# Hybrid decoder step on one core: steps moved to other places in the engines' hand-written order

## The chip, the cores and the metric

The kernel runs on one core of a Trainium2 chip. The metric is the device time of one launch in microseconds (us), lower is better. Engines as the profile names them: PE (TensorE, with PEld for its weight loads), DVE (VectorE), ACT (ScalarE), POOL (GpSimd) and SP (SyncE). Each runs its own list of instructions in the order in which the program wrote them; they meet only at semaphores. The core has 16 DMA engines.

## The reference, cut to what matters

One decoder layer over 1024 prompt tokens and 8 x 4 sample tokens, all in float32. A mixer (RMSNorm, input projection, a pooling half and a convolution half with 31 taps, LayerNorm, Silu, output projection, residual) comes first; then the expert retrieval, which is most of the time; then a gate with a per-layer embedding, and a last RMSNorm.

```python
def peer block(xk):                                   # 128 tokens
    q = (xk @ w_q).reshape(128, 8 heads, 2, 128)
    s = einsum('thpc,hpkc->thpk', q, sub_keys)
    sv, si = top_k(s, 16)                             # of 128 keys, for both halves
    cand = sv[:, :, 0, :, None] + sv[:, :, 1, None, :]
    top_s, top_j = top_k(cand.reshape(.., 256), 16)
    eidx = take_along_axis(si0 * 128 + si1, top_j)
    gate = softmax(top_s)
    h = gelu(einsum('td,thkd->thk', xk, u_tab[eidx]))  # rows of 1024 floats
    return einsum('thk,thkd->td', gate * h, v_tab[eidx])

h = h + peer(rmsnorm(h, g_ffn))
gate = sigmoid(rmsnorm(h, g_ple) @ w_ple_gate)
h = h + (p @ w_ple_proj) * gate
y = rmsnorm(h, g_final)
```

## The kernel before, in words

A first stage (`front`) runs the mixer for the first 512 prompt tokens and the sample tokens. The second stage (`experts`) does everything else. It walks through 66 blocks, numbered b, of 16 steps each, numbered k. A prompt block is one head of one tile of 128 tokens: block b = 8t + h, so blocks 0 to 63 are the eight prompt tiles, 64 and 65 the sample tokens, packed. A step is one chosen expert of each of the 128 tokens.

For step (b, k) POOL issues an indirect DMA that gathers 128 rows of `u_tab`, 4 KB each, into one of 8 buffers `u_row`, and DVE makes the dot product with the tokens (`dot`, L1772). After the 16 dots ACT makes the gelu of the block (L1277), DVE the coefficients (`coefficients`, L1763, called at k = 2 of the next block), ACT a diagonal matrix for each coefficient (L1188), and PE multiplies that diagonal by the gathered row of `v_tab`, adding in the PSUM bank `acc` (L1671). For a few steps DVE adds the row itself (L1790, `VECTOR_KS`).

POOL's order (L1064 to L1092) is a gather of u for step n, then a gather of v for step n - 20 (`V_BEHIND`). A u gather waits until the dot that used its buffer 8 steps earlier is done. A v gather waits until PE (or DVE) has used its buffer, which held the row 7 steps earlier (`V_RING`). So PE works about 20 steps behind DVE: PE at (b, k) stands level with DVE at (b + 1, k + 4).

When a tile t is complete, PE can't begin the next one in `acc` before `add_sum(t)` on DVE (L1781) has added it to the tokens: L1664 waits for `added`. The first row of tile t on PE is (8t, 0); its last row of the old tile is (8t - 1, 15).

In the gaps of this walk all other work is placed by hand. Tables such as `ADD_AT = {(17, 8): 0, ...}` say at which (b, k) of an engine's loop a step is written:

- The late mixer: the mixer for the other 512 prompt tokens runs within blocks 0 to 20. `LATE_OPEN`, `LATE_GATE`, `LATE_POOL` place steps of the convolution and pooling halves on DVE (`late_open` L1847, `late_gate`, `late_pool` L1873); `PROJECT_AT` the halves of the output projection on PE (L1530); `ADD_AT` the residual additions on DVE (L1926); `SQUARE_AT` their squares on ACT (L1245); four Silu stand at ACT (16, 0).
- Queries for the later tiles: PE multiplies (L1373), ACT copies, DVE picks the best 16 keys (`pick`, L1687 to L1697, called at k = 0 and k = 2).
- DVE ranks the next block's candidates at k = 4 (`rank_tile`, L1703 to L1726).
- The epilogues: `EPILOGUE` lists, for the eight prompt tiles e = 0 to 7, the block in which PE starts the gate of tile e: 40, 42, 44, 48, 50, 52, 59 and 64. PE makes the first half of the gate at k = 8, 11 and 14 of that block (L1429, L1434; for e = 7 at k = 4 and 6) and the second half in the next block. ACT takes the sigmoid of the first half at k = 1 of block + 1 and of the second at k = 8. DVE takes `mix_half` (L1823) of them at k = 7 and 14 of block + 2 and `finish` (L1832) in block + 3.

ACT's loop over b begins with the gelu of block b, which waits for the 16 dots of block b; then it makes the diagonals of block b, while DVE is in block b + 1.

## Time and profile before

| quantity | value |
|---|---|
| median of 3 runs | 3331.15 us (3305.53 to 3348.43) |
| the profiled execution | 3331.15 us |
| its span, first to last instruction | 3329.4 us |
| PE busy | 2669.7 us (80%) |
| DVE busy | 2273.8 us (68%) |
| ACT busy | 806.6 us (24%) |
| POOL busy | 2089.0 us (63%) |
| traffic | 1167.87 MB, of which the gathers 1107.43 MB, mean 351 GB/s |
| mean granted TensorE clock | 0.937 |

How to read it: busy counts the instructions' own time; an engine's idle time matters only where another waits for it. The rows of the timeline give start and duration in us, the engine, the line, the operation, what it writes and reads, the shape and the count of instructions merged; in brackets stands the idle time of the engine before it and what ended it. "remote" is an update that the profile can't assign.

### The profile page before, as it was taken

How to read it: one execution, taken by the hardware profiler on the slowest of the kernel's cores; microseconds unless marked ns; L12 is line 12 of the kernel's file. 1: busy time of each engine (PE TensorE's matmuls, PEld its weight loads, DVE VectorE, ACT ScalarE, POOL GpSimd, SP SyncE). 2: the span in 40 equal slices, each digit the busy share in tenths (PEclk: the TensorE clock that was granted, in tenths of full speed). 3: DMA queues.
4: the chain of work that ended last, by engine and by line, in shares of the span. 5: the costliest groups of instructions: out<-in, count | busy, mean ns of one | idle time of the engine just before them, and what ended most of it. 6: DMA issues, size and time to landing. Idle time of an engine off the chain costs nothing.

```text
span 3329.4 us, 24888 instructions
## 1 busy us (share of the span) xinstructions
PE 2669.7 (80%) x6723; PEld 1218.2 (37%) x6723; DVE 2273.8 (68%) x5244; ACT 806.6 (24%) x1938; POOL 2089.0 (63%) x2169
## 2 busy tenths in 40 slices
PE   8988888788978767677687887699878887778767
PEld 7753434333323323233343442233323333223322
DVE  8867777987875766786765756655566666555545
ACT  2332322223131212111212222222221222212212
POOL 2135666677766767566665666666666666666664
PEclk9998989999999989899898999999999899999899
DMA  5269999999999999899898999999999999999996
GB/s 146 68 223 344 381 369 380 376 392 371 397 367 379 390 372 375 303 379 379 326 383 335 368 366 409 387 373 375 378 372 374 370 371 371 375 373 369 373 367 225
DMA packets 363167, 1167.87 MB, mean 351 GB/s; under 512 B 35401, under 2 KB 88217, under 8 KB 363029
## 3 DMA queue, kind: packets, MB, share of 16 engines
q0 software_dynamic: 304128, 1107.43, 87.2%
q1 hardware_dynamic: 58368, 58.02, 5.3%
q8 instruction: 57, 0.93, 0.1%
q10 hardware_dynamic: 533, 0.83, 0.1%
q14 instruction: 81, 0.66, 0.1%
HBM read 1160.98 MB, written 5.15 MB: 350 GB/s over the span
## 4 chain that ended last, share of the span: by engine, by line
PE 24%; another core or an unknown queue 15%; POOL 14%; DVE 13%; issue 13%; DMA 11%; ACT 4%; POOLq 0%; DVEq 0%; ACTq 0%
PE ex_acc L1671 16%; POOL ex_v_row L1066 8%; POOL ex_u_row L1066 7%; DMA ex_u_row<-in_u_tab_dram,ex_eidx 6%; DMA ex_v_row<-in_v_tab_dram,ex_eidx 5%; DVE ex_u_row L1772 5%; PE ex_q L1373 2%; PE ex_turn L1429 1%; ACT ex_diag L1188 1%; DVE m_mix L1865 1%; PE ex_q L1429 1%; DVE m_hT L1790 1%; PE ex_turn L1510 1%; DVE ex_lists L1690 1%
## 5 line engine op out<-in xcount | busy, mean ns | idle before, releaser
L1671 PE MATMUL ex_acc<-ex_v_row,ex_diag 128*128 128x512 f32 x3840 | 1903.0, 637 | 570.3 <-DMA ex_v_row<-in_v_tab_dram,ex_eidx 252.4
L1772 DVE CUSTOM_DVE_ANT_0 ex_u_row<-ex_u_row,ex_xn 128x1024 f32<-128x1024 f32 x1056 | 1260.5, 1216 | 607.5 <-DMA ex_u_row<-in_u_tab_dram,ex_eidx 459.8
L1066 POOL DMA_INDIRECT ex_v_row<-in_v_tab_dram,ex_eidx x1024 | 996.3, 973 | 638.5 <-issue 260.7
L1671 PEld LDWEIGHTS ex_acc<-ex_v_row,ex_diag 128*128 128x128 f32 x3840 | 729.9, 201 | 1652.0 <-issue 1418.8
L1066 POOL DMA_INDIRECT ex_u_row<-in_u_tab_dram,ex_eidx x1024 | 988.7, 966 | 456.6 <-issue 289.4
L1188 ACT ACTIVATE ex_diag<-m_ident,ex_coef 128x128 f32<-128x128 f32 x948 | 320.2, 393 | 768.9 <-issue 314.3
L1373 PE MATMUL ex_q<-m_mix,m_wq 128*128 128x384 f32 (+3 forms) x832 | 238.5, 441 | 2.3 <-PEq L95 1.9
L1373 PEld LDWEIGHTS ex_q<-m_mix,m_wq 128*128 128x128 f32 x832 | 143.5, 194 | 101.9 <-issue 64.7
L1102 ACT COPY ex_qT<-ex_q 128x384 f32<-128x384 f32 (+3 forms) x50 | 22.0, 440 | 441.9 <-remote 305.2
L1112 ACT ACTIVATE ex_score<-ex_s,ex_rstd 128x128 f32<-128x128 f32 (+1 forms) x144 | 42.3, 364 | 237.6 <-remote 130.6
L1790 DVE SCALAR_TENSOR_TENSOR m_hT<-ex_v_row,ex_coef,m_hT 128x1024 f32<-128x1024 f32 x76 | 97.4, 1281 | 0.0
L1384 PE MATMUL ex_s<-m_keysT,ex_qT 128*128 128x128 f32 x288 | 49.8, 309 | 56.3 <-ACT ex_qT L1102 46.6
L1510 PE MATMUL ex_turn<-m_hT,m_wq 128*128 128x512 f32 x192 | 86.3, 592 | 0.0
L1772 DVE DVE_READ_ACCUMULATOR2_ANT ex_hdot<- 128x1 f32 x1056 | 85.6, 81 | 0.4 <-issue 0.4
L1277 ACT ACT_TABLE_LOAD x65 | 83.4, 1283 | 1.2
L1865 DVE SCALAR_TENSOR_TENSOR m_mix<-m_mix,m_taps 128x512 f32<-128x512 f32 x109 | 82.1, 753 | 0.0
L1118 ACT ACT_TABLE_LOAD x63 | 80.8, 1283 | 1.1
L1384 PEld LDWEIGHTS ex_s<-m_keysT,ex_qT 128*128 128x128 f32 x288 | 41.3, 202 | 88.6 <-ACT ex_qT L1102 59.2
L1277 ACT ACTIVATE ex_hact<-ex_hdot 128x16 f32<-128x16 f32 x66 | 14.2, 216 | 239.8 <-issue 122.8
L1429 PE MATMUL ex_turn<-m_mix,m_wq 128*128 128x512 f32 x128 | 60.3, 615 | 6.2 <-ACT m_wq L1142 6.2
L1694 DVE MAX8 ex_lists<-ex_same 128x8 f32<-128x128 f32 (+1 forms) x144 | 32.7, 281 | 41.0 <-remote 28.0
L1429 PE MATMUL ex_q<-m_mix,m_wq 128*128 128x512 f32 x128 | 57.7, 594 | 0.0
(371 smaller groups left out, 1968.0 us busy)
## 6 DMA issues: line engine op xcount, KB each, us to landing
m_wq<-in_w_q_dram SPq DMA_DIRECT2D x18, 1024.0 KB
ex_u_row<-in_u_tab_dram,ex_eidx POOLq DMA_INDIRECT x1024
ex_v_row<-in_v_tab_dram,ex_eidx POOLq DMA_INDIRECT x1024
fr_w<-in_w_in_dram SPq DMA_DIRECT2D x12, 512.0 KB, 4.4
m_wq<-in_w_in_dram SPq DMA_DIRECT2D x6, 1024.0 KB
m_wq<-in_w_out_dram SPq DMA_DIRECT2D x4, 1024.0 KB
m_mix<-in_w_ple_gate_dram SPq DMA_DIRECT2D x8, 512.0 KB
out_y_prompt_dram<-m_wq SPq DMA_DIRECT2D x7, 512.0 KB
```

The source lines that it names most:

```text
L1066: pool.indirect_dma_start(out=row[:, :], out_offset=None, in_=table, in_offset=bass.IndirectOffsetOnAxis(ap=picks(b)[:, k:k + 1], axis=0)) ...
L1118: nc.scalar.activation(expo[r % KEPT][:, :], shift[r % 2][:, :], ACT.Exp, accum_out=norm[r % KEPT][:, :]).then_inc(exped, 1)
L1188: nc.scalar.activation(diag[:, n % DIAGS, 0:rows(t)], pattern[:, :], ACT.Copy, scale=coef[b % 2][:, k:k + 1]).then_inc(diaged, 1)
L1277: nc.scalar.activation(hact[b % 2][:, :], hdot[b % 2][:, :], ACT.Gelu_apprx_tanh).then_inc(gelued, 1)
L1373: last = nc.tensor.matmul(q_ps[:, out:out + cols], weights(load, c), xg[:, c, at:at + cols], start=(c == 0), stop=(c == DC - 1))
L1384: last = nc.tensor.matmul(s_ps[0:rows(t), j * P:(j + 1) * P], qT[:, s % 2, j * P:j * P + rows(t)], keysT[:, half, :], start=True, stop=True)
L1429: last = nc.tensor.matmul(gate_out[:, :], x2T[:, c, :], w_gate[:, c, cols], start=(c == 0), stop=(c == DC - 1))
L1510: last = nc.tensor.matmul(late_bank[n % 2], weights(late_load(n), c), late_h[:, c, :], start=(c == 0), stop=(c == DC - 1))
L1671: last = nc.tensor.matmul(acc[0:rows(t), half, :], diag[:, tensor_sums(n) % DIAGS, 0:rows(t)], row[:, half * HALF_D:(half + 1) * HALF_D], ...
L1772: nc.vector.tensor_tensor_reduce(out=u_row[n % U_RING][:, :], in0=u_row[n % U_RING][:, :], in1=xn[:, :], scale=1.0, scalar=0.0, op0=ALU.mu ...
L1790: ins = nc.vector.scalar_tensor_tensor(out=tokens, in0=row[:, :].rearrange("p (c e) -> p c e", c=DC), scalar=coef[b % 2][:, k:k + 1], in1= ...
L1865: nc.vector.scalar_tensor_tensor(out=u, in0=src, scalar=tap[:, j:j + 1], in1=u, op0=ALU.mult, op1=ALU.add).then_inc(late_tapped, 1)
```

## The change

All edits move steps to other (b, k) places; what a step computes stays. `add_sum(t - 1)` goes from k = 5 to k = 2 of the second block of a tile, behind the coefficients and ahead of the second pick. The sigmoid of the first gate half goes from k = 1 of block + 1 to k = 15 of the epilogue's own block, on ACT, behind the block's last diagonal and ahead of the next block's gelu. `mix_half` goes from k = 7 and 14 to 3 and 12, `take_spread` from 14 to 11. In the late mixer `LATE_OPEN`, `LATE_GATE` and `LATE_POOL` move up by one or two steps in the entries shown, the additions by 3 to 5 steps, the squares by 2 to 6, the four Silu from ACT (16, 0) to (15, 15), three halves of the projection by 1 or 2 steps.

```diff
-LATE_OPEN = ((8, 0), (9, 10), (11, 14), (13, 4))
-LATE_GATE = ((8, 5), (9, 15), (12, 3), (13, 9))
-LATE_POOL = ((10, 6), (10, 14), (13, 14), (14, 8))
+LATE_OPEN = ((8, 0), (9, 10), (11, 13), (13, 2))
+LATE_GATE = ((8, 5), (9, 15), (12, 2), (13, 7))
+LATE_POOL = ((10, 6), (10, 14), (13, 12), (14, 6))
-PROJECT_AT = {(15, 5): (0, 0), (15, 9): (1, 0), (16, 3): (0, 1), (16, 6): (1, 1), (16, 8): (2, 0), ...
+PROJECT_AT = {(15, 5): (0, 0), (15, 9): (1, 0), (16, 1): (0, 1), (16, 4): (1, 1), (16, 7): (2, 0), ...
-ADD_AT = {(17, 8): 0, (17, 11): 1, (17, 15): 2, (18, 6): 3, (18, 12): 4, (19, 2): 5, (19, 9): 6, (19, 15): 7}
-SQUARE_AT = {(16, 11): 0, (16, 14): 1, (17, 2): 2, (17, 9): 3, (17, 15): 4, (18, 5): 5, (18, 12): 6, (19, 1): 7}
+ADD_AT = {(17, 3): 0, (17, 6): 1, (17, 12): 2, (18, 3): 3, (18, 9): 4, (18, 15): 5, (19, 6): 6, (19, 12): 7}
+SQUARE_AT = {(16, 6): 0, (16, 9): 1, (16, 14): 2, (17, 6): 3, (17, 12): 4, (18, 2): 5, (18, 9): 6, (18, 14): 7}
@@ ACT, late_step
-                if (b, k) == (16, 0):
+                if (b, k) == (15, 15):
                     for c in range(MC):
@@ ACT, the loop over blocks
                         if k == TURN_AT[e][1] + 1 and e < N_TILES - 1:
                             embedding_out(e)
-                    if rest_e is not None and k == 1:
-                        sigmoid_half(rest_e, 0)
+                        if k == TOPK - 1:
+                            sigmoid_half(e, 0)
@@ DVE, late_step
-                if (b, k) == (20, 6):
+                if (b, k) == (20, 2):
                     late_sum_squares(DC - 1)
@@ DVE, the loop over blocks
                         if b - 1 in VECTOR_KS:
                             dve.wait_ge(coefed, b)
-                    if k == 5 and t > 0 and h == 1:
-                        add_sum(t - 1)
+                        if t > 0 and h == 1:
+                            add_sum(t - 1)
                     if k == 0 and s is not None:
                         pick(s)
...
-                    if k == 14 and t == N_TILES - 1 and h == 2:
+                    if k == 11 and t == N_TILES - 1 and h == 2:
                         take_spread()
                     dot(b, k)
...
-                    if mix_e is not None and k == 7:
+                    if mix_e is not None and k == 3:
                         mix_half(mix_e, 0)
-                    if mix_e is not None and k == 14:
+                    if mix_e is not None and k == 12:
                         mix_half(mix_e, 1)
                         add_mixed(mix_e)
```

## Rows read from the trace of the kernel before

**Rows 1.** Busy time by windows: us; PE, PEld, DVE, ACT, POOL; PEclk; DMA share, GB/s.
```profile
217.00:3266.00 3049.00, 2424.79 (x5700) 1045.69 (x5699) 2069.81 (x4833) 720.27 (x1743) 2020.01 (x2087) 0.93 0.97 371
627.00:1178.00 551.00, 461.83 (x1005) 189.97 (x1004) 426.34 (x801) 143.00 (x344) 385.67 (x383) 0.95 1.00 384
1005.00:1035.00 30.00, 24.43 (x53) 10.82 (x54) 17.42 (x28) 4.51 (x9) 17.55 (x19) 0.84 0.90 334
1382.00:1412.00 30.00, 15.90 (x50) 8.55 (x50) 23.83 (x44) 2.83 (x9) 12.84 (x14) 0.77 0.68 244
1770.00:1800.00 30.00, 16.02 (x47) 8.62 (x48) 20.24 (x41) 3.38 (x11) 12.29 (x14) 0.72 0.66 233
...
3240.00:3305.00 65.00, 46.00 (x92) 13.35 (x92) 37.42 (x45) 10.45 (x21) 39.01 (x36) 0.84 0.86 307
```

**Rows 2.** Waits of the whole program: who waited for whom, us, times, longest.
```profile
POOL ex_v_row L1066 <- PE ex_acc L1671: 232.4, 129, 9.3
...
POOL ex_u_row L1066 <- DVE ex_hdot L1772: 78.9, 79, 5.7
```

**Rows 3.** Timeline where tile 2 begins (block 17).
```profile
999.62 2.50 PE L1671 MATMUL ex_acc<-ex_v_row,ex_diag 128*128 128x512 f32 x4 [1.96 <-issue]
1010.57 6.95 PE L1671 MATMUL ex_acc<-ex_v_row,ex_diag 128*128 128x512 f32 x11 [8.45 <-remote]
...
993.63 0.23 DVE L1763 SCALAR_TENSOR_TENSOR ex_coef<-ex_expo,ex_norm,ex_hact 128x16 f32<-128x16 f32 x1
...
1005.60 1.21 DVE L1781 TENSOR_TENSOR m_hT<-m_hT,ex_acc 128x1024 f32<-128x1024 f32 x1
```

**Rows 4.** Timeline where tile 3 begins (block 25).
```profile
1369.93 0.23 DVE L1763 SCALAR_TENSOR_TENSOR ex_coef<-ex_expo,ex_norm,ex_hact 128x16 f32<-128x16 f32 x1
...
1374.16 1.96 PE L1671 MATMUL ex_acc<-ex_v_row,ex_diag 128*128 128x512 f32 x4 [0.60 <-DMA ex_v_row<-in_v_tab_dram,ex_eidx]
...
1375.95 5.32 PE L1373 MATMUL ex_q<-m_mix,m_wq 128*128 128x384 f32 x16
...
1378.95 0.48 DVE L1694 MAX8 ex_lists<-ex_same 128x8 f32<-128x128 f32 x2 [6.09 <-remote]
...
1385.94 1.22 DVE L1772 CUSTOM_DVE_ANT_0 ex_u_row<-ex_u_row,ex_xn 128x1024 f32<-128x1024 f32 x1 [4.29 <-remote]
...
1388.83 0.93 POOL L1066 DMA_INDIRECT ex_u_row<-in_u_tab_dram,ex_eidx  x1 [5.66 <-DVE ex_hdot L1772]
...
1396.10 5.75 PE L1671 MATMUL ex_acc<-ex_v_row,ex_diag 128*128 128x512 f32 x8 [14.83 <-DVE m_hT L1781]
...
1400.15 0.94 POOL L1066 DMA_INDIRECT ex_v_row<-in_v_tab_dram,ex_eidx  x1 [7.91 <-PE ex_acc L1671]
```

**Rows 5.** Timelines of two epilogues: block 44 (the first two rows), block 52.
```profile
2269.81 0.23 DVE L1763 SCALAR_TENSOR_TENSOR ex_coef<-ex_expo,ex_norm,ex_hact 128x16 f32<-128x16 f32 x1
...
2273.30 1.88 PE L1434 MATMUL ex_turn<-m_keysT,ex_qT 128*128 128x512 f32 x4
...
2637.09 0.23 DVE L1763 SCALAR_TENSOR_TENSOR ex_coef<-ex_expo,ex_norm,ex_hact 128x16 f32<-128x16 f32 x1
...
2645.75 1.88 PE L1434 MATMUL ex_turn<-m_keysT,ex_qT 128*128 128x512 f32 x4
...
2647.53 1.21 DVE L1772 CUSTOM_DVE_ANT_0 ex_u_row<-ex_u_row,ex_xn 128x1024 f32<-128x1024 f32 x1
...
2658.15 0.94 POOL L1066 DMA_INDIRECT ex_u_row<-in_u_tab_dram,ex_eidx  x1 [0.30 <-issue]
```

**Rows 6.** Timeline where the sample tokens begin (block 65).
```profile
3232.41 1.95 PE L1671 MATMUL ex_acc<-ex_v_row,ex_diag 128*128 128x512 f32 x4 [1.36 <-issue]
...
3240.97 1.22 DVE L1781 TENSOR_TENSOR m_hT<-m_hT,ex_acc 128x1024 f32<-128x1024 f32 x1 [6.16 <-remote]
```

**Rows 7.** The page's groups: the table load ahead of the gelu; busy, mean ns, idle.
```profile
L1277 ACT ACT_TABLE_LOAD x65 | 83.4, 1283 | 1.2
```

**Rows 8.** One line's account: what DVE waited for ahead of L1926, us, times.
```profile
  remote: 30.4, 3
```

More of the change, by code:

```diff
@@ L790 @@
 TAP_ADD_AT = (15, 7)
-PROJECT_AT = {(15, 5): (0, 0), (15, 9): (1, 0), (16, 3): (0, 1), (16, 6): (1, 1), (16, 8): (2, 0), (16, 10): (2, 1), (16, 13): (3, 0),
+PROJECT_AT = {(15, 5): (0, 0), (15, 9): (1, 0), (16, 1): (0, 1), (16, 4): (1, 1), (16, 7): (2, 0), (16, 10): (2, 1), (16, 13): (3, 0),
               (17, 1): (3, 1), (17, 4): (4, 0), (17, 7): (4, 1), (17, 10): (5, 0), (17, 13): (5, 1), (18, 1): (6, 0), (18, 4): (6, 1),
               (18, 7): (7, 0), (18, 10): (7, 1)}
-ADD_AT = {(17, 8): 0, (17, 11): 1, (17, 15): 2, (18, 6): 3, (18, 12): 4, (19, 2): 5, (19, 9): 6, (19, 15): 7}
-SQUARE_AT = {(16, 11): 0, (16, 14): 1, (17, 2): 2, (17, 9): 3, (17, 15): 4, (18, 5): 5, (18, 12): 6, (19, 1): 7}
+ADD_AT = {(17, 3): 0, (17, 6): 1, (17, 12): 2, (18, 3): 3, (18, 9): 4, (18, 15): 5, (19, 6): 6, (19, 12): 7}
+SQUARE_AT = {(16, 6): 0, (16, 9): 1, (16, 14): 2, (17, 6): 3, (17, 12): 4, (18, 2): 5, (18, 9): 6, (18, 14): 7}
 def col(t):
```

## The prediction

> **What bounds the kernel now.** Read the table by windows first. From the first dot of the expert stage at 217 us to the last at 3266 us, 1056 rows of u and nearly as many of v are gathered, and the DMA engines are busy 0.97 of the time at 371 GB/s; PE is busy 2425 and VectorE 2070 of those 3049 us [rows 1]. So the gathers set the pace, 3049/1056 = 2.9 us for a pair of rows, and a change of schedule can give back only time in which they were not fed: at most 0.03 of 3049, about 91 us, and part of that is how a saturated stretch reads. See there too how uneven the idle time is: 1.00 over the whole late mixer stage, 0.68 and 0.66 in two stretches of 30 us.
>
> Then the waits: who stops feeding the DMAs? POOL issues every gather. It waited 232 us for PE to free a v buffer and 79 us for a dot to free a u buffer [rows 2]. So the buffers are the clock, and PE's progress counts for more than VectorE's.
>
> Then the timelines at the low stretches. At each new tile of tokens PE must not start its sum before VectorE has taken the old sum out of acc (L1781). In a common case PE ends its last row at 1002.1, VectorE adds at 1005.6, PE resumes at 1010.6 after 8.45 us of idleness [rows 3]. At tile 3 it is worse: PE ends its row at 1376.1 and runs a query; VectorE is held in its second pick (waits of 6.09 and 4.29 us), makes two dots and a ranking and then adds, 1.2 us before PE resumes at 1396.1 after 14.83 us idle. POOL pauses 5.66 us for the dot and 7.91 us for PE [rows 4]. The stretch 1382:1412 loses (0.97 - 0.68) x 30 = 8.7 us against the mean, 1770:1800 (tile 4) 9.3 and 1005:1035 (tile 2) 2.1 [rows 1]. The 13.6 us of POOL pauses thus cost 0.64 us of DMA time each.
>
> The releases of some waits come microseconds after the record of the releasing instruction ended (VectorE's 6.09 us wait in a chain of its own instructions [rows 4]). I can't name the cause; it goes into the range.
>
> **The change, part by part.** No instruction is added or removed; every edit moves a step, with its waits, to another place in its engine's order. No DMA is issued from a moved step, and POOL's and SP's orders stay.
>
> *add_sum from k = 5 to k = 2.* v row (8t-1, 15), the last of the old tile, is issued behind u row (8t+1, 3), since v lags by 20 rows. VectorE at k = 2 is therefore early and waits for PE: in [rows 3] from 993.9, the end of the coefficients, to 1002.1, so 8.2 us, then adds 1.2. Its dots 2 and 3 and the ranking come later, and the dots have room: POOL issues the gather that reuses a buffer several us after its dot, 9.4 us in the row pair of [rows 5] (dot (52,4) ends 2648.7, the gather into its buffer starts 2658.15). An 8.2 us delay just fits, so a common seam costs nothing in dots and frees PE 3 to 7 us sooner. What it can win is only what the stretch lost, 2.1 us at tile 2, and no other of tiles 1, 5, 6 and 7 has a low stretch of this kind; together I take 2 us of gain (0 to 4).
> At tile 3, and tile 4 alike, the add would start at 1376.1 instead of 1394.9; PE's query (to 1381.3) hides it, PE resumes 14.8 us sooner and the 7.91 us pause goes. What is late next is dot 2, now behind the add: the pick began right behind the coefficients, at 1370.2, and would begin behind the add, at 1377.3, 7.1 us later. Without its two long waits (10.4 us) the dot comes at 1382.6, before POOL stopped (1383.2), and the 5.66 us pause goes too (all 8.7 us back); stretched as before, it comes at 1393.0, the pauses sum to 12.8 instead of 13.6 and 0.5 us comes back. Nothing before shows this order, so I take the middle, 5 us, twice: 10 us (1 to 18).
> At tile 8 PE ends its last row at 3234.4 and the add is at 3241.0, 6.6 us later [rows 6]. Behind it hang the last epilogue and the last sums, and 3240:3305 loses (0.97 - 0.86) x 65 = 7.2 us [rows 1]. I take 4 us (0 to 7.2).
>
> *The first sigmoid half from (block+1, k = 1) to (block, k = 15).* This speaks against the change. It now stands ahead of the next block's gelu on ScalarE, and it waits for PE's gate product. Behind the gelu wait the coefficients on VectorE at k = 2, and behind those its dots. In epilogue 4 the coefficients were made at 2637.1 and the gate product ended at 2647.6; with a gelu table load of 1.28 [rows 7] and 1.2 for the sigmoid, the gelu and the hand-overs (each a short activation, my estimate from the 0.7 us of a 128x512 step) they can't come before 2650.1, 13.0 us later. Room at dot 4 was 9.4, and mix_half at k = 3 takes 0.7 of it: POOL pauses 4.3 us more. In epilogue 1 the gate ends at 2275.2, the coefficients were at 2269.8, and the shift is 7.9 us: inside the room [rows 5]. Three of the seven are of the long kind, the rest near the short one. PE meets the next block's first diagonal two rows behind the gate, some 3 us, so it is hardly late itself. Cost: 0 if the pauses fall where POOL waits for PE anyway, 3 x 4.3 x 0.64 = 8 us if none does; I take 3. In the last epilogue the sigmoid ahead of the last gelu is harmless only if the tile-8 add is early.
> At this point the Trainium skill (ScalarE: Activation LUTs, What ACT_TABLE_LOAD costs) says that a switch of tables takes a 1.28 us load and a 1.38 us drain. The trace agrees on the load (1283 ns [rows 7]); no row here shows the drain. By the page each shift would be an estimated 1.4 us longer, and the sum 3 x 1.4 x 0.64 = 3 us higher.
>
> *mix halves to k = 3 and k = 12, take_spread to k = 11.* The first can't wait, since its sigmoid precedes the coefficients. The others come two or three rows before PE has worked them off, up to 8 us of VectorE waiting inside the same room: 0.
>
> *The late mixer's places.* Adds, squares, openings and pools come one to five rows earlier; PE's products hardly move. PE at row (b, k) is level with VectorE at (b+1, k+4). An add for the product at PE (16, 1) is thus due at (17, 5); it stood at (17, 8) and now stands at (17, 3), so VectorE waits two pairs more, 5.8 us, eight times over. The three longest such waits before summed to 30.4 us [rows 8], and the DMAs still ran at 1.00 of 627:1178 [rows 1]. Nothing can be gained at 1.00. Cost 0 to 6 us (one pair at two of its places); I take 2. If that cover is gone each add costs its wait.
>
> Sum: -(2 + 10 + 4) + 3 + 2 = -11. The profiled execution took 3331.15 us, its span 3329.4, and it is the median of the runs shown. Forecast 3320.
>
> **The rivals.**
> *No gain.* The pick is as stretched as before, so dot 2 takes the place of PE as POOL's wait at tiles 3 and 4 (2 us gained), the other terms give 3, the costs of 5 stand: 3331. For it: the two waits of 6.09 and 4.29 us came in the middle of a burst of gathers that would still be there.
> *All of it.* Seams 8.7 + 9.3 + 4, the end 7.2, no cost: 29 us, 3302. For it: PE's wait is much the larger part of what POOL waits for; against: every cost would have to be covered.
> *Slower: the gelu behind the gate.* If the room at the dots is 5 us and not 9.4, because POOL, no longer held by PE, asks for buffers earlier, then three long shifts of 13 and four of 8 pause POOL 3 x 8 + 4 x 3 = 36 us, x 0.64 = 23 us. Less 16 and plus 2 for the late stage: 3340. It decides from a room of about 7 us. With no room at all it would be 71 x 0.64 = 45 us, 3362.
> *VectorE's catching up stops the gathers.* After each longer wait VectorE runs some 8 dots of 1.2 us back to back, at 15 places. If no gather could be issued beside them, that is 15 x 9.7 x 0.64 = 93 us, 3424 less the gains. Against it: the gathers issued in [rows 4, 5] take 0.93 or 0.94 us though VectorE is busy two thirds of the time [rows 1]. This is the Trainium skill's rule of the shared port (SBUF - State Buffer, A bandwidth-pool intuition that's wrong): a descriptor write waits till a two-port VectorE operation has ended. The trace does not show it here.
>
> **How the numbers follow.** Forecast 0.45, no gain 0.22, all of it 0.15, the gelu 0.15, catching up 0.03. The likeliest case's own range is 3308 to 3331. The three runs before span 3305.5 to 3348.4, so scatter of a median is itself a dozen us, as large as the effect; that and the two middle rivals give 3288 to 3345. Two per cent is 67 us, about what a measurement of this kernel can tell from no change. No bound of the gains reaches that (29 us); the last rival does. Faster by over 2% 0.02, within 0.95, slower 0.03.
>
> **What would show it.** PE's idle time ahead of each tile's first row shrinks from 5 to 15 us to under 5, and at tiles 3 and 4 it is the query that ends it. The DMA share of the two low stretches rises from 0.67 to 0.8 or more; if it stays, see whether POOL waits for the dot. The wait of the coefficients at epilogue block + 2 grows from nothing to 8 to 13 us: if POOL's waits for dots grow from 79 us by more than 20, the slower rival is at work. VectorE's waits at L1926 grow well above 30 us with the share in the late stage still 1.00. The forecast is wrong if that share falls to 0.97, or if the last row of the old tile is itself late.

## The result, and the profile after

The changed kernel takes 3346.15 us (median of 21 runs, 3313.93 to 3364.1), the kernel before 3329.36 (21 runs, 3289.47 to 3351.99). The ratio is 1.0053, with a 95% interval of 1.0031 to 1.0076: 17 us slower, within 2%. The forecast was 3320 with a range of 3288 to 3345. It missed the range by 1 us and, more important, the sign: the gains of the sum are not there and its costs are larger. Executions more than 1.5% above the fastest of their kernel are left out of the ratios here and below, among them one of 8291 us in e13 and one of 5529 us in e16. The profiled execution took 3370.4 us (span 3368.6), 24 us above the median of its kernel, so its totals are not to be read as the size of the effect.

The table by windows of the changed kernel, for the stretches of [rows 1] (us; PE, PEld, DVE, ACT, POOL busy; PEclk; DMA share, GB/s):

```profile
217.00:3303.00 3086.00, 2448.02 (x5700) 1049.95 (x5699) 2063.70 (x4832) 728.01 (x1750) 2027.08 (x2087) 0.93 0.97 367
632.00:1192.00 560.00, 462.72 (x1005) 190.34 (x1005) 428.10 (x803) 142.37 (x345) 384.73 (x384) 0.96 0.98 377
1015.00:1045.00 30.00, 28.61 (x66) 12.42 (x67) 21.95 (x45) 4.03 (x11) 18.64 (x20) 1.00 1.00 390
1403.00:1433.00 30.00, 19.33 (x53) 9.77 (x51) 21.83 (x43) 6.47 (x18) 16.44 (x17) 0.83 0.88 327
1800.00:1830.00 30.00, 20.30 (x61) 10.41 (x59) 21.13 (x55) 4.39 (x15) 19.30 (x22) 0.89 0.98 366
3278.00:3343.00 65.00, 48.10 (x89) 13.49 (x90) 39.54 (x50) 11.73 (x22) 39.76 (x35) 0.76 0.84 292
```

The low stretches behind the seams (a seam is the passage from one tile to the next) filled up, as announced: 0.90 became 1.00 at tile 2, 0.68 became 0.88 at tile 3, 0.66 became 0.98 at tile 4. The late mixer's stretch went the other way, from 1.00 and 551 us to 0.98 and 560 us. Next the waits of POOL in the changed kernel, to be held against [rows 2] (us in total, times, longest):

```profile
POOL ex_v_row L1066 <- remote: 172.4, 70, 4.4
POOL ex_u_row L1066 <- DVE ex_hdot L1772: 157.4, 99, 12.0
POOL ex_v_row L1066 <- PE ex_acc L1671: 147.2, 97, 4.8
```

POOL's waits for PE fell by 85 us and its waits for dots grew by 79. That is not an even exchange: its waits of L1066 for a v buffer that the profile gives as "remote" grew as well, from 139.8 to 172.4 us, so the v side gained 53 us and the dots took 79. All of POOL's pauses longer than 0.5 us in the expert stage, summed from the trace, went from 447 to 482 us, and the two profiled spans lie 39 us apart. VectorE shows where it comes from: in the same table for VectorE the coefficients (L1763) now wait 70.6 us in 10 waits (longest 15.5) and 31.2 in 5 more, the adds (L1781) 52.8 us in 5 (longest 17.4), 16.8 in one and 7.8 in 2.

### The profile page after: what moved, and what is told of

The parts are those of the page before. It is cut to its first block, busy times and chain, and to the rows that moved or that the text cites. A ratio compares the mean times of both kernels' runs of the same rounds, so it can differ in the third digit from the quotient of the medians.

```text
span 3368.6 us, 24895 instructions
## 1 busy us (share of the span) xinstructions
PE 2698.3 (80%) x6723; PEld 1222.9 (36%) x6723; DVE 2268.0 (67%) x5244; ACT 815.5 (24%) x1946; POOL 2097.5 (62%) x2169
## 4 chain that ended last, share of the span: by engine, by line
PE 22%; DVE 19%; POOL 15%; issue 13%; another core or an unknown queue 13%; DMA 10%; ACT 2%; DVEq 0%; POOLq 0%; ACTq 0%
PE ex_acc L1671 14%; DVE ex_u_row L1772 8%; POOL ex_v_row L1066 8%; POOL ex_u_row L1066 7%; DMA ex_u_row<-in_u_tab_dram,ex_eidx 5%; DMA ex_v_row<-in_v_tab_dram,ex_eidx 4%; PE ex_q L1373 3%; PE ex_turn L1429 2%; DVE m_mix L1865 1%; PE ex_q L1429 1%; DVE m_hT L1790 1%; DVE ex_lists L1697 1%; DVE ex_lists L1690 1%; DVE ex_same L1691 1%
## 5 line engine op out<-in xcount | busy, mean ns | idle before, releaser
L1066 POOL DMA_INDIRECT ex_v_row<-in_v_tab_dram,ex_eidx x1024 | 995.2, 972 | 598.1 <-issue 271.8
L1066 POOL DMA_INDIRECT ex_u_row<-in_u_tab_dram,ex_eidx x1024 | 996.0, 973 | 527.4 <-issue 285.2
L1763 DVE SCALAR_TENSOR_TENSOR ex_coef<-ex_expo,ex_norm,ex_hact 128x16 f32<-128x16 f32 x64 | 15.2, 238 | 117.9 <-issue 70.6
```

The source lines that it names most:

```text
L1066: pool.indirect_dma_start(out=row[:, :], out_offset=None, in_=table, in_offset=bass.IndirectOffsetOnAxis(ap=picks(b)[:, k:k + 1], axis=0)) ...
```

## The experiments

Each run is timed in five rounds against the kernel before on the same chip. A ratio of 0.1% is 3.3 us. The four parts of the change are called the add (add_sum at k = 2), the sigmoid, the mix (mix halves and take_spread) and the late part.

### The parts, each alone and in pairs

e1_add has only this edit:

```diff
-                    if k == 5 and t > 0 and h == 1:
-                        add_sum(t - 1)
+                        if t > 0 and h == 1:      # at k == 2
+                            add_sum(t - 1)
```

> One part alone: add_sum at k = 2 instead of k = 5, all else as before. The changed kernel is 17 us slower than before (ratio 1.0053) although PE's idle time at the seams went. Theory A (the add holds VectorE): at k = 2 VectorE stands in L1781 for up to 17 us while the dots 2 to 5 wait behind it, u buffers come free late and POOL waits for dots instead of for PE; POOL's wait for dots grows from 79 us by 20 or more, its wait for PE falls, and this part alone is 5 to 15 us slower. Theory B (the gelu behind the gate, my own slower rival): this part alone gains, -16 to 0 us, since the seams of tiles 3 and 4 are fed. Theory C (the late mixer): this part alone lies within 5 us of before.

Measured: ratio 0.9986 (0.9956 to 1.0016). POOL's waits for dots did grow, from 79 to 105 us, but the time didn't.

e2_epilogue has the sigmoid and the mix:

```diff
-                    if rest_e is not None and k == 1:
-                        sigmoid_half(rest_e, 0)
+                        if k == TOPK - 1:
+                            sigmoid_half(e, 0)
-                    if mix_e is not None and k == 7:
+                    if mix_e is not None and k == 3:
```

> The epilogue's edits alone: the first sigmoid half at (block, k = 15), the mix halves at k = 3 and k = 12, take_spread at k = 11; add_sum and the late mixer as before. Theory B (the gelu behind the gate): the coefficients' wait at each epilogue block + 2 grows from nothing to 8 to 15 us, POOL's wait for dots grows by 20 us or more, and this part carries the whole loss, 15 to 30 us slower. Theory A (the add holds VectorE): 0 to 5 us. Theory C (the late mixer): 0 to 5 us.

Measured: 1.0015 (0.9981 to 1.0048). The coefficients' waits came (7.1 to 12.6 us at the seven epilogues), the 15 us of the one theory did not.

e3_late has the tables of the late mixer, and the add at k = 2 for block 17 alone:

```diff
-ADD_AT = {(17, 8): 0, (17, 11): 1, (17, 15): 2, (18, 6): 3, ...
+ADD_AT = {(17, 3): 0, (17, 6): 1, (17, 12): 2, (18, 3): 3, ...
+                        if t in (2,) and h == 1:
+                            add_sum(t - 1)
```

> The late mixer's new places, with add_sum at k = 2 at the seam of block 17 alone, because the first late addition at (17, 3) waits for a product that PE makes behind its wait for that add; all other seams and the epilogues as before. Theory C (the late mixer): the waits of L1926 and the squares hold VectorE and ScalarE between blocks 16 and 20, the share of the DMAs over blocks 13 to 20 falls from 1.00 to 0.98 or less, and this part is 8 to 17 us slower. Theories A and B: 0 to 5 us.

Measured: 1.0008 (0.997 to 1.0045), less than the 8 us that were expected at least, though the interval doesn't exclude them.

e4_add_epilogue is the changed kernel without the late part.

> add_sum at k = 2 and the epilogue's edits together, the late mixer as before: the whole change without its late part. If the parts add up, this is the sum of the two runs of one part, and the change's 17 us less what the late part costs. Theory C: 0 to 8 us slower. Theories A and B: 12 to 20 us slower. A fourth theory, that the two delays work only together (a late add in the block behind a late gelu uses up the same room), expects each part alone within 5 us and this one 15 us slower.

Measured: 1.0014 (0.9981 to 1.0047).

No part stands out by its time, since a part is worth as much as the interval is wide. But one place in the profiles does. Between blocks 16 and 22 (POOL's issue of the u row of the one to that of the other) the kernels without the late part took 276.8, 273.6, 276.4 and 275.0 us, those with it 283.1 (changed kernel) and 289.8 (e3). That made the late part the first suspect, and three of the next four runs test it. (The profile of e3 fell on one of its longest executions, 3360.8 us against a median of 3345.2, so its 289.8 is an upper end.)

### The late additions: again, taken back, made earlier still

e5_after_again is the changed kernel, unchanged.

> The changed kernel once more, as the reference for the two runs beside it. So far: POOL's wait for dots between blocks 16 and 20 is 1.5 to 2.7 us in the four profiles without the late mixer's new places and 14.4 and 25.5 us in the two with them, and those five blocks last 5 and 14 us longer. Late-mixer theory: here too POOL's wait for dots there is over 10 us, the five blocks last 5 to 15 us longer than in the kernel before, and the time is 8 to 20 us above it. If chance made that pattern, the wait is under 5 us in this profile.

Measured: 1.0045 (1.0011 to 1.008), 15 us slower, a second time. But here blocks 16 to 22 took 273.7 us and POOL waited 1.8 us for dots between blocks 16 and 20: the loss in that place does not come in every execution.

```diff
# e6_adds_back, against the changed kernel
-ADD_AT = {(17, 3): 0, (17, 6): 1, (17, 12): 2, (18, 3): 3, (18, 9): 4, (18, 15): 5, (19, 6): 6, (19, 12): 7}
+ADD_AT = {(17, 8): 0, (17, 11): 1, (17, 15): 2, (18, 6): 3, (18, 12): 4, (19, 2): 5, (19, 9): 6, (19, 15): 7}
# e7_adds_earlier, against the changed kernel
+ADD_AT = {(17, 2): 0, (17, 4): 1, (17, 10): 2, (18, 2): 3, (18, 7): 4, (18, 13): 5, (19, 4): 6, (19, 10): 7}
```

> The changed kernel with the late additions (L1926) and their squares (L1245) back at the places of before; the products, openings, gates and pools of the late mixer stay at their new ones, and so do all other edits. If the additions' waits for the products are the cost: POOL's wait for dots between blocks 16 and 20 falls back under 5 us, ScalarE's waits for the additions fall, those blocks last as long as before, and the time falls 8 to 15 us below the changed kernel's. If it is the products or the openings: both stay as in the changed kernel.

Measured: 1.0021 (0.999 to 1.0052); blocks 16 to 22 took 277.8 us, POOL waited 2.4 us for dots between blocks 16 and 20.

> The changed kernel with the late additions 1 to 2 row pairs earlier still, and their squares with them: the suspected cost made larger. If VectorE's wait for the products is the cost, its waits at L1926 grow by 8 x 3 to 6 us, POOL's wait for dots between blocks 16 and 20 grows to 30 us or more, and the time is a further 10 to 25 us up, 25 to 45 us above the kernel before. If the additions cost nothing, the time is within 5 us of the changed kernel's.

Measured: 1.0067 (1.0039 to 1.0095), 22 us slower. That is 5 to 7 us above the changed kernel's two ratios, within the intervals, and short of the 25 us and more that were expected; POOL's wait for dots between blocks 16 and 20 was 16.7 us and not 30. Blocks 16 to 22 took 294.8 us. The windows of blocks 16 to 22 in e4 (late part as before), in e12 (below: late part as changed) and in e7, same columns as above:

```profile
933.00:1208.00 275.00, 220.20 (x470) 89.71 (x468) 187.20 (x348) 66.77 (x146) 188.63 (x192) 0.93 1.00 383
```

```profile
937.00:1224.00 287.00, 223.59 (x472) 90.35 (x471) 186.57 (x347) 68.18 (x148) 190.09 (x192) 0.92 0.97 367
```

```profile
947.00:1242.00 295.00, 226.19 (x475) 90.70 (x473) 189.05 (x353) 68.14 (x148) 189.55 (x193) 0.92 0.94 354
```

The same 192 gathers in 275, 287 and 295 us, with a share of 1.00, 0.97 and 0.94. How it happens stands in the timeline of the changed kernel at block 18. L1530 on PE, 8 matmuls, is the half product that the addition of (18, 3) waits for:

```profile
1064.13 3.60 PE L1530 MATMUL ex_turn<-m_mix,m_wq 128*128 128x512 f32 x8
...
1073.05 0.94 POOL L1066 DMA_INDIRECT ex_v_row<-in_v_tab_dram,ex_eidx  x1 [0.30 <-issue]
1077.79 0.69 DVE L1926 TENSOR_TENSOR m_hT<-m_hT,ex_turn 128x512 f32<-128x512 f32 x1 [18.17 <-remote]
1078.51 0.63 ACT L1245 ACTIVATE m_mix<-m_hT 128x512 f32<-128x512 f32 x1 [20.38 <-DVE m_hT L1926]
1085.95 0.93 POOL L1066 DMA_INDIRECT ex_u_row<-in_u_tab_dram,ex_eidx  x1 [11.96 <-DVE ex_hdot L1772]
```

The addition at (18, 3) waits 18.17 us. Behind it on VectorE stand the dots, so POOL, whose last gather was at 1073.05, stops for 11.96 us; behind it on ScalarE stands the square (20.38 us), and behind that the diagonals. But PE had ended the product at 1067.7, 8.1 us into the wait. The other 10.1 us passed with the product done: the release came late. In e5, the same program, it came at once (product to 1071.97, addition at 1072.00):

```profile
1068.37 3.60 PE L1530 MATMUL ex_turn<-m_mix,m_wq 128*128 128x512 f32 x8
...
1072.00 0.69 DVE L1926 TENSOR_TENSOR m_hT<-m_hT,ex_turn 128x512 f32<-128x512 f32 x1 [6.42 <-issue]
```

There blocks 16 to 22 took 273.7 us, as in the kernels without the late part. In e12 and e3 the same addition waited 18.0 and 15.8 us, of which 9.7 and 7.7 us came after the product's end, and the blocks took 287.3 and 289.8. So the new places bring a wait of some 8 us, and it is the late release on top that makes a loss. In e7, whose places are earlier still, the waits without any late release are themselves up to 11.6 us. The addition n = 3 can't stand much earlier than it does: its product is made at PE (17, 1), which needs the coefficients that VectorE makes at (18, 2), one step ahead of (18, 3).

### What a held engine costs

e8_seams_later was meant to lengthen PE's idleness at five seams.

```diff
-                    if k == 5 and t > 0 and h == 1:
+                    if k == (5 if t in (1, 2, N_TILES - 1) else 8) and t > 0 and h == 1:
```

> The kernel before with add_sum at k = 8 instead of k = 5 at the seams of tiles 3 to 7: PE stands three row pairs, some 8.7 us, longer at each of five seams, 44 us in all. It measures what PE's idleness at a seam costs. By the step of the forecast (0.64 us of DMA time for each us that POOL pauses, all of it turned into pauses) it would be 28 us slower, with a low DMA stretch at each of the five seams; if the buffers cover most of it (which would also explain that taking the idleness away brings nearly nothing) it is 0 to 10 us slower.

Measured: 1.0 (0.997 to 1.0031). It decides nothing: VectorE works off dots 5 to 7 in 1.2 us each once it is behind, and PE's idleness ahead of the first rows summed to 74.8 us. The first profile has 70.9, but the others with all adds at k = 5 and no held engine have 54.9 (e2), 53.7 (e11), 52.5 (e14) and 75.9 (e15), in the mean of the five 61.6: this sum too differs from execution to execution by more than the edit changed it. The price had to be measured by holding the engine itself.

```diff
# e9_pe_held: PE, 8 seams
+                    for half in [0, 1] * 4 if h == 0 and k == 0 and t > 0 else []:
+                        nc.tensor.matmul(acc[0:rows(t), half, :], diag[...], row[...], start=True, stop=True)
# e10_vector_held (7) and e13_vector_held_twice (15): VectorE, 8 tile starts
+                    for _ in range(7 if t > 0 else 0):
+                        chain.step(nc.vector.scalar_tensor_tensor(out=xn[...], ...))
```

> The kernel before, with the first row of each of the tiles 1 to 8 multiplied four times more before it is summed: 8 matmuls on PE, 7.8 us at each seam, 62 us in all, and nothing else. It measures the price of PE's time at a seam, which the run with add_sum at k = 8 did not (VectorE worked off its dots there and PE stood only 6 us longer in all). By the step of the forecast (0.64 us for each us that POOL pauses for PE, nothing between PE's delay and POOL's pause) it is 40 us slower, with low DMA stretches at all eight seams. If the v buffers and PE's spare fifth of the time take it up, it is 0 to 12 us slower, and then the idleness that the change removed from the seams was worth nothing either.

Measured: 1.0078 (1.0043 to 1.0113). The added products in the page's groups of e9 (busy, mean ns):

```profile
L1671 PE MATMUL ex_acc<-ex_v_row,ex_diag 128*128 128x512 f32 (+1 forms) x128 | 73.2, 736 | 58.5 <-issue 25.7 <-DVE m_hT L1784 24.2 <-ACT ex_diag L1188 8.6
```

73.2 us of PE cost 26 us (14 to 38): 0.36 us per us (0.2 to 0.5), so neither the 40 us of the one expectation nor the 0 to 12 of the other.

> The kernel before, with the scaled tokens of each of the tiles 1 to 8 computed seven times more: VectorE is held some 9 us longer at each of eight tile starts, 70 us in all. It measures the price of holding VectorE once, as the early adds and the late coefficients of the change do. By the forecast (room of 9.4 us at the dots) it costs about nothing, 0 to 5 us. If the room is 5 us or less, POOL waits for dots 4 us or more at each of the eight, and it is 15 to 40 us slower.

Measured: 1.0003 (0.9983 to 1.0023), for 8 x 7 x 1.293 = 72 us of VectorE: nothing that the measurement can tell.

> The kernel before, with the scaled tokens of the tiles 1 to 8 computed 15 times more: VectorE is held 18 to 19 us at each of eight tile starts, about the longest waits that the changed kernel shows (12 to 18 us at L1781, L1763 and L1926). Holding it 9 us cost 1 us in all. If the dots have a room of some 9 us and no more, each place costs (18.5 - 9.4) x 0.4 to 0.64 us, 30 to 45 us in all, and POOL's wait for dots grows by 70 us; this would explain why long waits of VectorE eat what PE gains. If VectorE can be held at will, it is 0 to 5 us slower.

Measured, over five executions: 1.0178 (1.0131 to 1.0225), 60 us slower (44 to 76), for 8 x 15 x 1.295 = 155 us. The page's groups of e10 for the repeated operation (7 x 7 in tiles 1 to 7; the sample tile's stand in a group of their own), and then POOL's wait for dots in it (us, times, longest):

```profile
L1961 DVE SCALAR_TENSOR_TENSOR ex_xn<-m_hT,ex_rstd,ex_g_ffn 128x1024 f32<-128x1024 f32 x49 | 63.4, 1293 | 7.5 <-ACT m_hT L1123 5.6
```

```profile
POOL ex_u_row L1066 <- DVE ex_hdot L1772: 92.3, 66, 5.9
```

The same two views of e13 (15 x 7):

```profile
L1961 DVE SCALAR_TENSOR_TENSOR ex_xn<-m_hT,ex_rstd,ex_g_ffn 128x1024 f32<-128x1024 f32 x105 | 136.0, 1295 | 4.0
```

```profile
POOL ex_u_row L1066 <- DVE ex_hdot L1772: 176.5, 90, 12.7
```

So VectorE may be held 9.1 us at a place for nothing, and 19.4 us at the same places cost 60 us. If all of that stems from what is beyond 9.1 us, it is 60 / (8 x 10.3) = 0.73 us per us. The curve bends: in proportion, e10 would have cost 28 us. Where between 9.1 and 19.4 us it bends isn't shown; if no us of holding costs more than one us, it is below 14 us. The room of 9.4 us that the forecast read from one buffer in [rows 5] agrees with it. POOL's waits for dots grew by 98 us over the kernel before in e13, 0.61 us of time for each, near the forecast's 0.64.

### Which of the rest costs

e11_products moves PE's late products alone; e12_no_epilogue is the changed kernel without the sigmoid and the mix; e14 and e15 are the sigmoid alone and the mix alone; e16 has the add at k = 4.

> The kernel before with the late mixer's three products of PE at their new places and the additions where they were: the part of the change that should shorten the wait at the additions. The changed kernel with the additions put back ran blocks 16 to 20 in 225.0 us, the kernels without late edits in 229.3 to 234.4, those with all of them in 234.8 to 246.0. Expected if that holds: 225 us here too, POOL's wait for dots there under 5 us, and the time 0 to 8 us below the kernel before; otherwise those blocks last 229 to 234 us and the time is the same.

Measured: 1.0007 (0.9985 to 1.003); blocks 16 to 22 took 273.8 us, as without it, and blocks 16 to 20 228.8, not 225. The products' places show no gain and no cost.

> The changed kernel without the epilogue's edits: all eight adds at k = 2 and all of the late mixer's places. Late-mixer theory: blocks 16 to 20 last over 234 us, and the time is 8 to 17 us above the kernel before. If the epilogue's edits carry a part of the loss (blocks 40 to 65 last 1134.8 to 1143.7 us without them and 1136.9 to 1144.8 with them, which does not tell), this run is 4 us or more faster than the changed kernel, 4 to 10 us above before.

Measured: 1.002 (0.9994 to 1.0047), 7 us, as expected if the epilogue's edits carry a part; blocks 16 to 22 took 287.3 us. The later runs without the late part took 273.7 to 279.3 us there (e8 to e11, e14, e16), but e15 281.2 and e13, whose VectorE is held at block 16, 288.0. The length of these blocks alone therefore doesn't mark the late part; the late release at (18, 3) does.

> The kernel before with the first sigmoid half at (block, k = 15) alone, ahead of the next gelu: the part that the forecast named as speaking against the change. If it carries the epilogue's cost, the coefficients wait 8 to 15 us at each epilogue block + 2, POOL's waits for dots grow, and the time is 5 to 12 us above the kernel before; the mix halves then cost nothing.

Measured: 1.0016 (0.9987 to 1.0045), 5 us, at the lower end of what was expected, with an interval that includes nothing at all. The coefficients of e14 waited for the gelu as in the changed kernel (VectorE's waits, us, times, longest):

```profile
DVE ex_coef L1763 <- ACT ex_hact L1277: 60.5, 12, 14.4
...
DVE ex_coef L1763 <- issue: 35.1, 6, 15.7
```

> The kernel before with the mix halves at k = 3 and k = 12 and take_spread at k = 11, the sigmoids where they were. If the waits at these places cost (6 us at most in the changed kernel, 16 us at take_spread), this run is 5 to 12 us above the kernel before; if the sigmoid half carries the cost, it is within 3 us of it.

Measured: 1.0019 (0.9989 to 1.005), 6 us, between the two expectations and with an interval that covers both.

> The kernel before with add_sum at k = 4 instead of k = 5, the middle between it and the change. At k = 2 VectorE waited 6 to 18 us at each seam and PE's idleness fell from 71 us to 38; at k = 5 VectorE hardly waits. If the loss of the early place is VectorE's hold, k = 4 keeps a part of PE's gain at waits under 9 us: 0 to 8 us faster than before. If PE's time at the seams is worth nothing, it is the same.

Measured: 1.0001 (0.9964 to 1.0038). PE's idleness at the seams is 37.8 us here too, and no gain can be seen; by e9's price the 24 us less than the mean with k = 5 would be worth 9 us, which the interval doesn't exclude. Six of VectorE's eight waits at the adds were 3.3 us or less, the other two 9.6 and 12.2, with the release 7.5 and 10.1 us behind PE's last row.

Taken together the runs say more than each alone. A sum of parts, fitted by least squares with each run's interval as its weight (the changed kernel twice, e1 to e4, e6, e12; sigmoid and mix as one part; e11 for the products, taken as neutral), gives: the add -2 us (-9 to +5), the sigmoid and the mix +8.5 (+2 to +15), the late additions +8.7 (+2 to +15). The sum is 15 us, and no run lies more than 0.18% from it. It takes for granted that the parts add up and that the runs are independent, though the runs of a set share their executions of the kernel before; the uncertainties are therefore at least these. e14 and e15 with a term each give +4 and +5 us, both with 8 us of uncertainty: whether the sigmoid or the mix carries the epilogue's cost stays open.

### The unchanged kernel twice more

> The kernel before, unchanged, once more: a second execution's profile. If the low stretches at tiles 3 and 4 belong to the program, PE stands 14 to 15 us at both seams again and the DMAs lose some 9 us in each. If they come and go, PE's idleness at the two differs by 5 us or more from 14.8 and 14.6, and the DMA time lost in blocks 25 and 33 together is nearer the 9 to 15 us of the other kernels with the same code there than the 19.9 us of the first profile.

> The same, a third execution's profile. The expectations are those of the second.

Both, one execution each, came out on another chip than all others, and there the unchanged program takes 3082.67 us, 7 to 8% less. The windows of e17, the whole expert stage and the two stretches behind the seams of tiles 3 and 4:

```profile
217.00:3025.00 2808.00, 2366.80 (x5725) 1011.87 (x5724) 2079.16 (x4832) 726.66 (x1743) 2023.67 (x2090) 0.98 1.02 404
1293.00:1323.00 30.00, 25.58 (x76) 12.74 (x74) 27.52 (x63) 5.38 (x18) 20.55 (x22) 0.94 0.97 363
1637.00:1667.00 30.00, 26.59 (x80) 13.70 (x81) 23.42 (x61) 4.40 (x14) 20.36 (x22) 1.00 0.99 378
```

So they answer the question for that chip only. A share of 1.02 and 404 GB/s instead of 0.97 and 371, and no low stretches: 0.97 and 0.99 where the first profile has 0.68 and 0.66. PE stood 3.26 and 0.96 us at the two seams, not 14.83 and 14.6 (e17, both tiles):

```profile
1307.16 1.32 PE L1671 MATMUL ex_acc<-ex_v_row,ex_diag 128*128 128x512 f32 x2 [3.26 <-DVE m_hT L1781]
...
1651.44 1.98 PE L1671 MATMUL ex_acc<-ex_v_row,ex_diag 128*128 128x512 f32 x4 [0.96 <-DVE m_hT L1781]
```

The other chip alone would leave open whether this is the chip or the draw. e11 settles it for the chips of the comparison: it has the old add and the old epilogue, and at tile 4 PE went from its row over the query straight on, with no idleness, and the share was 0.98; at tile 3 it was 0.76. In e2, too, PE stood 0.0 us at tile 4 and 14.9 at tile 3.

```profile
1756.88 5.32 PE L1373 MATMUL ex_q<-m_mix,m_wq 128*128 128x384 f32 x16
1762.04 1.52 PE L1671 MATMUL ex_acc<-ex_v_row,ex_diag 128*128 128x512 f32 x3
```

```profile
1373.00:1403.00 30.00, 18.27 (x54) 9.44 (x54) 24.70 (x45) 6.47 (x18) 14.61 (x16) 0.77 0.76 269
1743.00:1773.00 30.00, 27.43 (x65) 12.91 (x66) 24.44 (x67) 8.37 (x23) 18.22 (x20) 0.90 0.98 367
```

## Why the prediction failed, step by step

**The reading of what bounds the kernel was right.** The gathers set the pace, and an engine's time counts only through a pause of POOL. e9, e10 and e13 agree with it and give a price for each.

**The step that failed: the late releases were put at nothing in the sum.** The forecast saw that some releases come microseconds after the releasing instruction has ended, and left this to the range. Its sum then took an 8.2 us wait of VectorE as one that "just fits" 9.4 us of room. The waits that it described were there: counted up to the moment when PE's last row was done, the 56 waits at the adds of the seven kernels with k = 2 are at most 11.0 us, and six are above 9.1. As measured, with the late release on top, they reach 18.5 us. The same holds for the late additions. It is the moved steps that are exposed to it, since they now wait where they had arrived after the release.

**The seams' gain (2 + 10 + 4 = 16 us) was the largest error; measured, 2 us with 7 of uncertainty.** The mechanics came as described: PE resumed within 1.4 us at six of eight seams of the changed kernel (idle 1.4, 1.4, 0, 0, 1.3, 1.3, then 10.3 and 8.5 us), behind the query at tiles 3 and 4, and the low stretches filled. Three things explain the missing gain.

First, the term of 10 us was sized from one execution. The DMA time lost in blocks 25 and 33 together, summed from the records in steps of 1 us, was 19.9 us in the first profile; in the seven profiles that keep the add at k = 5 there (that one, e2, e3, e8, e11, e14, e15) it is 13.8 us in the mean, 9.2 to 19.9; in the seven with k = 2 it is 9.1, 6.5 to 12.5. The first profile was the worst draw of the seven, and what the edit gives back at both tiles is 4.7 us, less than half of the term.

Second, the price. The step "0.64 us of DMA time for each us that POOL pauses" skips the link before it: PE's delay has first to become a pause. For PE's own time e9 has 0.36. The seven kernels with k = 2 have 30.1 us of PE idleness at the seams in the mean, the five with k = 5 have 61.6; at 0.36 the difference is worth an estimated 11 us.

Third, what replaced it. VectorE has to stand at the seam until PE's release arrives. The forecast took 8.2 us for that, within the room of 9.4. In e1 the eight waits were 5.4, 9.9, 7.5, 15.6, 14.0, 18.5, 7.5 and 16.1 us, five of them beyond 9.1 us, one of them twice as long as the room. Up to PE's last row they were 5.3, 9.8, 4.8, 8.8, 7.4, 6.9, 7.4 and 7.1. The seam of tile 6 in e1:

```profile
2492.58 1.96 PE L1671 MATMUL ex_acc<-ex_v_row,ex_diag 128*128 128x512 f32 x4 [0.61 <-DMA ex_v_row<-in_v_tab_dram,ex_eidx]
2494.46 0.94 POOL L1066 DMA_INDIRECT ex_u_row<-in_u_tab_dram,ex_eidx  x1 [0.31 <-issue]
...
2506.18 1.22 DVE L1781 TENSOR_TENSOR m_hT<-m_hT,ex_acc 128x1024 f32<-128x1024 f32 x1 [18.53 <-remote]
...
2507.46 3.48 PE L1671 MATMUL ex_acc<-ex_v_row,ex_diag 128*128 128x512 f32 x4 [12.92 <-DVE m_hT L1781]
2508.82 0.94 POOL L1066 DMA_INDIRECT ex_u_row<-in_u_tab_dram,ex_eidx  x1 [7.06 <-DVE ex_hdot L1772]
```

PE's last row ended at 2494.5. VectorE stood ready since 2487.7 and began its add at 2506.2, 11.6 us after the row it waited for. PE, which was to be freed, stood 12.92 us, longer than the 5.2 us before, and POOL 7.06. With the add at k = 5 the release had come when VectorE arrived at this seam in the first profile, and its lateness cost nothing. What the seven kernels with k = 2 waited beyond 9.1 us is 17.7 us in the mean (9.1 to 28.6); without the late releases it would be 0.8. At e13's 0.73 it costs an estimated 13 us, against the 11 us above: together about the measured nothing. e13 held VectorE at another place, the start of the tile's first block, so this balance is an estimate and not shown; in e1 alone, where it would come out at some 12 us of loss, the measured time does not bear it out.

**The sigmoid ahead of the gelu (3 us) was described rightly and weighed too low.** The coefficients' waits at the seven epilogues of the changed kernel were 12.2, 7.6, 7.9, 9.7, 12.1, 15.5 and 13.7 us, against 8 and 13 foretold, and the chain from the end of the gate product to the coefficients took 2.4 us (estimated 2.5) at six of the seven; at the first PE's release came 4.3 us late. So in this profile the waits themselves are long, nearly without late releases. What was beyond 9.1 us sums to 17.7 us; at 0.73 that is 13 us. The forecast had 8 us for the case that nothing covers the pauses, 0 for full cover, and took 3. The measured 8.5 (with the mix) is at the uncovered end. Of the Trainium skill's 1.38 us drain beside the 1.28 us table load (ScalarE: Activation LUTs, What ACT_TABLE_LOAD costs) the trace shows nothing: in the changed kernel's epilogue of block 50 the sigmoid starts at 2675.11 and takes 0.69, the load starts at 2675.81, and the gelu at 2677.11.

**The mix at no cost** is not refuted and not confirmed (e15: +0.19%, with 0.3% of uncertainty).

**The late part (2 us) costs 8.7.** The forecast priced it as two pairs more of waiting, 5.8 us at a time, in a stage whose share of 1.00 could give nothing and, so it seemed, lose little. But the waits there are not all lengthened alike: their sum went only from 37 to 43 us. One or two of the eight become very long (18.2 us in the changed kernel, 18.0 in e12, 15.8 and 15.1 in e3), because a release 7.6 to 10.1 us late comes on top of a wait of some 8, and a single one of them stops POOL for 12 us. Before, a release came as late (8.4 us behind the product of n = 4), but VectorE arrived only when that product was nearly done and waited 8.8 us in all. The mark that I had set for being wrong, a share of 0.97 in the late stage, came near with 0.98 over 632:1192. [rows 8] gave the sum of waits and not the longest, which is what mattered. How much of the 8.7 us the late releases make is not measured by a run; e5's time was 15 us above the kernel before although its profiled execution lost nothing in these blocks.

**The rivals.** "No gain" at 3331 had the seams right and the costs too low (it also counts the other seam gains as 3, where the sum has 6, without saying why); "the gelu behind the gate" at 3340 is nearest to the result, and for the right reason in half of it: dots held beyond their room. Its premise, a room of 5 us, does not fit e10, where 9.1 us of holding cost nothing that can be told. The late part is the other half and was no rival's. "All of it" and "VectorE's catching up" are out: e10 and the changed kernel are full of catching up, and in e10 it costs nothing.

**No version here beats the kernel before** on the chips of the comparison: e1 and e16 are level with it.

## What to carry to other kernels

Here a wait was harmless while it was shorter than the room behind it, and cost much of its length beyond. So before a step is moved up to where it must wait, look at the longest wait that it may meet, not at the mean or the sum. If releases in the trace come late, add their lateness to the wait: a wait that just fits its room does not fit. Put steps that wait for another engine where their condition has long been met. A low stretch of one profile is a draw, that is, it differs from execution to execution: before a gain is sized from it, see whether neighbours of the same kind or a second profile show it too. Here the same code at tile 4 lost 9 us of DMA time in the first profile and next to nothing in e11's.

## What the runs showed of the hardware that was not expected

**Releases that come late, on some chips.** In the seven kernels with the add at k = 2 the adds waited for PE 56 times in all. 29 of them began 0.0 to 0.6 us after PE's last row had ended (or VectorE's own last instruction, if later), 24 began 2 to 12 us after it, 3 in between. PE's late products show the same (block 18 above). A prompt one, tile 2 of the changed kernel (PE's row ends at 1014.01):

```profile
1012.05 1.96 PE L1671 MATMUL ex_acc<-ex_v_row,ex_diag 128*128 128x512 f32 x4 [1.54 <-DMA ex_v_row<-in_v_tab_dram,ex_eidx]
...
1014.09 1.22 DVE L1781 TENSOR_TENSOR m_hT<-m_hT,ex_acc 128x1024 f32<-128x1024 f32 x1 [9.21 <-issue]
```

The recorded semaphore updates themselves are late there: PE's update for the row that ended at 2494.5 is recorded at 2506.16, and VectorE starts at 2506.18, so it is not the waiting engine that sleeps. On the chip of e17 this is nearly absent. In the first profile, from the first dot on, some 460 of PE's 882 recorded updates stand more than 0.5 us behind the last ended instruction that could have made them, in e17 30 of 1173; and the waits "remote" of POOL, 139.8 us in 60 waits in the first profile, don't occur in e17's table, which goes:

```profile
POOL ex_v_row L1066 <- PE ex_acc L1671: 190.8, 260, 7.3
...
POOL ex_u_row L1066 <- DVE ex_hdot L1772: 61.7, 162, 3.2
```

(The first trace also has fewer updates recorded for the same program, so these shares are rough.) What makes the releases late isn't settled. Gathers in close succession are not enough: at all 29 prompt adds POOL was issuing back to back too, and went on for 5 us or more. It comes with the lower DMA rate, and PE's and VectorE's updates show it (VectorE 188 of 1249, in e17 45 of 2541), ScalarE's hardly (some 35 of 635, in e17 some 30 of 1380).

**The same program at 404 and at 371 GB/s.** The median of the kernel before was 3329 to 3356 us in five sets of runs on at least three chips (one chip gave 3335 and 3353 in two sets); on the chip of e17 and e18 it took 3078.37 and 3082.67 us. The Trainium skill (Perfetto Trace Analysis, Roofline) says that a core's share of the memory bandwidth is 358 GB/s when both cores of a pair access it, and that one alone can draw more, up to some 435. Both of this case's figures lie above that share and below that limit. Whether a neighbour was at work on the slower chips no run here shows. In e17 blocks 0 to 64 lose some 14 us of DMA time in all, against some 130 in the first profile, so the change could hardly gain anything there; it wasn't run on it.
